# First attention of a two-block network on Trainium2: scores contracted over 128, 128 and 32 rows in place of three times 96

## The reference, cut to what matters

```
kv = (rms_norm(u_kv) @ w_kv_up);  k_nope, v = split(kv)        # 64 + 64 for each of 8 heads
q_rope = apply_rope(q_rope, cos, sin);  k_rope = apply_rope(u_kr, cos, sin)   # 32 features
s = einsum("bqhd,bkhd->bhqk", q_nope, k_nope) + einsum("bqhd,bkd->bhqk", q_rope, k_rope)
p = softmax(s * scale);   o = einsum("bhqk,bkhd->bqhd", p, v)
```

## Time and profile before

| | us |
|---|---|
| median of 3 runs (2778.56 to 2780.07) | 2779.03 |
| the profiled execution's own time | 2780.26 |
| its span, first to last instruction | 2778.3 |
| PE busy (98% of the span) | 2726.2 |
| DVE busy (65%) | 1800.1 |
| ACT busy (45%) | 1259.2 |
| POOL busy (16%) | 439.2 |

### The profile page before, as it was taken

The page is one execution under the profiler, slowest core; times in us unless marked ns, Lnnn a source line. Parts: engine busy times, 40 slices in busy tenths (PEclk is TensorE's granted clock), DMA queues, the critical chain, the costliest instruction groups (busy, mean ns, idle before and its releaser), DMA issues.

```text
span 2778.3 us, 36356 instructions
## 1 busy us (share of the span) xinstructions
PE 2726.2 (98%) x14436; PEld 2281.4 (82%) x14436; DVE 1800.1 (65%) x2497; ACT 1259.2 (45%) x2026; POOL 439.2 (16%) x393
## 2 busy tenths in 40 slices
PE   8999999999999999999999999999999999999998
PEld 7978888788884888888888887878888868888898
DVE  3646888330546888888885968988886572110575
ACT  4333787141432777777776124454454453111101
POOL 1500231000011211111102000000001043221341
PEclk9999999999999999999999999999999999999999
DMA  4041000420217999999982121030121221110141
GB/s 140 31 154 46 31 1 1 165 93 32 92 67 294 391 396 396 396 396 396 395 326 69 61 104 49 20 118 28 60 72 42 94 76 46 46 46 31 60 145 61
DMA packets 141604, 379.79 MB, mean 137 GB/s; under 512 B 11952, under 2 KB 45234, under 8 KB 141309
## 3 DMA queue, kind: packets, MB, share of 16 engines
q1 hardware_dynamic: 126140, 325.22, 30.9%
q0 software_dynamic: 12560, 42.74, 4.9%
q10 hardware_dynamic: 2736, 9.50, 0.9%
HBM read 341.13 MB, written 35.26 MB: 135 GB/s over the span
## 4 chain that ended last, share of the span: by engine, by line
PE 91%; DVE 4%; ACT 2%; DMA 1%; issue 1%; POOL 0%; SPq 0%; ACTq 0%; POOLq 0%; DVEq 0%
PE ps L2988 8%; PE ps L2989 8%; PE ps L2990 8%; PE ps L2591 7%; PE ps L2973 6%; PE ps L2975 6%; PE ps L2974 6%; PE ps L3082 3%; PE ps L3084 3%; PE ps L3083 3%; PE ps L2605 3%; PE ps L3129 2%; PE ps L3094 1%; PE ps L3096 1%; PE ps L3095 1%; PE ps L3114 1%
## 5 line engine op out<-in xcount | busy, mean ns | idle before, releaser
L2310 DVE SCALAR_TENSOR_TENSOR b_f<-b_f,small_f 128x1023 f32<-128x1023 f32 (+14 forms) x240 | 304.3, 1268 | 27.0 <-ACT small_f L1279 13.8
L2988 PE MATMUL ps<-x_f32r,w_f32r 128*128 128x512 f32 x480 | 187.9, 392 | 4.3 <-DVE b_f L2507 3.6
L2990 PE MATMUL ps<-x_f32r,w_f32r 128*128 128x512 f32 x480 | 187.4, 390 | 0.0
L2974 PE MATMUL ps<-w_f32r,a_f32r 128*128 128x512 f32 x456 | 177.4, 389 | 0.0
L2989 PE MATMUL ps<-ht_f32r,w_f32r 128*128 128x512 f32 x416 | 162.5, 391 | 0.0
L3083 PE MATMUL ps<-w_f32r,a_f32r 128*128 128x512 f32 x384 | 149.9, 390 | 0.0
L2974 PE MATMUL ps<-x_f32r,a_f32r 128*128 128x512 f32 x312 | 121.4, 389 | 0.0
L1279 ACT ACTIVATE x_f<-ps 128x512 f32<-128x512 f32 (+1 forms) x184 | 91.0, 533 | 44.4 <-PE ps L2591 21.0
L1209 POOL TENSOR_TENSOR w_f32r<-w_f,w_f32r 128x2048 fp32r<-128x2048 f32 x23 | 110.2, 4793 | 1.9
L2988 PEld LDWEIGHTS ps<-x_f32r,w_f32r 128*128 128x128 f32 x480 | 90.4, 188 | 23.7 <-issue 4.9
L2990 PEld LDWEIGHTS ps<-x_f32r,w_f32r 128*128 128x128 f32 x480 | 90.5, 189 | 18.9
(11 more groups left out here) (578 smaller groups left out, 7870.6 us busy)
## 6 DMA issues: line engine op xcount, KB each, us to landing
w_f<-in_w_exp_up SPq DMA_DIRECT2D x40, 1024.0 KB, 10.3
w_f<-in_w_exp_down SPq DMA_DIRECT2D x38, 1024.0 KB, 10.2
w_f<-in_w_exp_gate SPq DMA_DIRECT2D x36, 1024.0 KB, 8.8
x_f<-in_w_exp_gate SPq DMA_DIRECT2D x28, 1024.0 KB, 8.6
x_f<-in_w_exp_down SPq DMA_DIRECT2D x26, 1024.0 KB, 11.0
x_f<-in_w_exp_up SPq DMA_DIRECT2D x24, 1024.0 KB, 10.3
w_f<-in_w_in SPq DMA_DIRECT2D x22, 1024.0 KB, 5.1
w_f<-in_w_in SPq DMA_DIRECT2D x10, 2048.0 KB, 8.1
```

The costliest lines, as they stand in the source:

```text
L2310: ins = v.scalar_tensor_tensor(C_conv[k][:, d:S], U_conv[k][:, 0:S - d], cols[:, k, R_TAP + j:R_TAP + j + 1], C_conv[k][:, d:S], ALU.mult, ...
L2974: mm(o, x1, w2[:, k, c], start=False, stop=False)
L2988: mm(o, l1, r1, start=(k == 0), stop=False)
L2990: ins = mm(o, l2, r1, start=False, stop=(k == n - 1))
```

## The change

The same 288 rows of products for each score are laid out anew. The first matmul contracts 128 rows: the high query's nope rows twice, against the key's low nope rows (rows 0 to 63) and its high nope rows (64 to 127). The second contracts 128 rows: the query's low nope rows and twice its high rope rows, against the key's high nope rows and its high and low rope rows. The third contracts 32 rows: the query's low rope rows (`r_lo`) against the key's high rope rows (`s_hi`), which lie four times in `s_hi`, at partitions 0, 32, 64 and 96. The two matmuls of 32 rows of a step stand at different partitions (0 and 32 for an even head, 64 and 96 for an odd one) and write to different banks. In the built program they carry a tile size of 32 rows by 128 columns, where the others have 128 by 128.

The second copies of high rows are made by transfers between places of the on-chip memory (`upper`, `lower`, `doubled`). POOL makes 14 copies of 32 by 512 in place of 2 of 32 by 3584. ACT and DVE split the rotated queries for all heads at once (`rope_round` and the loop behind it).

```diff
         def head_parts(nm, h):
             if nm == "k":
-                return KT[:, h, :], k_hi[h % 2], KT_lo[:, h, :]
-            return QT[:, h, :], q_hi[h % 2], QT_lo[:, h, :]
+                return KT[:, h, :], (k_hi[h % 2][0:NOPE, :], k_both[NOPE:P, h, :]), k_both[0:NOPE, h, :]
+            return QT[:, h, :], (q_hi[h % 2][0:NOPE, :], q_hi[h % 2][NOPE:P, :]), q_rest[0:NOPE, h, :]
@@ SP, under "mkv0"
-                    for j in range(2):
-                        sp.wait_ge(sem("q_rope"), j + 1)
-                        for m in range(2):
-                            sp.dma_start(QT[...head 0, half j...], rope_out[m][0:16, c]).then_inc(sem(f"q_first{j}"), 16)
+                    sp.wait_ge(sem("q_rope"), 4)
+                    def upper(h, name):
+                        for m in range(2):
+                            for r in (NOPE, NOPE + ROPE):
+                                sp.dma_start(value(q_rest[r + 16 * m:r + 16 * m + 16, h, :]), value(rope_hi[m][16 * h:16 * h + 16, :])).then_inc(sem(name), 16)
+                    def lower(h, name):
+                        for m in range(2):
+                            for r in (NOPE * (h % 2), NOPE * (h % 2) + ROPE):
+                                sp.dma_start(value(r_lo[h // 2][r + 16 * m:r + 16 * m + 16, :]), value(rope_lo[m][16 * h:16 * h + 16, :])).then_inc(sem(name), 16)
+                    upper(0, "q_first"), lower(0, "q_first")
                     for h in range(1, H1):
-                        (2 transfers of QT's rope rows, q_rest)
+                        upper(h, "q_rest")
+                    sp.wait_ge(sem("q_first"), 16 * 8)
+                    sp.wait_ge(sem("q_rest"), 16 * 4 * (H1 - 1))
+                    for h in range(1, H1):
+                        lower(h, "q_rest")
+                    def doubled(h):
+                        for j in range(2):
+                            sp.wait_ge(sem("head_hi"), 2 * h + 2 + j)
+                            lower_rows, upper_rows = head_parts("kq"[j], h)[1]
+                            sp.dma_start(value(upper_rows), value(lower_rows)).then_inc(sem("q_rest"), 16)
+                    doubled(1), doubled(2)
                     bk.wait(sp, ("s1", 2 * T - 1))
                     (2 transfers of w_out)
+                    for h in range(3, H1):
+                        doubled(h)
@@ POOL
+            bk.wait(pool, ("vt", T - 1))
             for j in range(2):
                 bk.read(pool, ("kr", j))
-                nc.gpsimd.tensor_copy(KT[NOPE:HD1, 1:H1, c], ...).then_inc(sem("k_rope"), 1)
+                for r in range(ROPE, P, ROPE):
+                    nc.gpsimd.tensor_copy(s_hi[r:r + ROPE, c], value(s_hi[0:ROPE, c]))
+                for i in range(2):
+                    nc.gpsimd.tensor_copy(k_hi[i][NOPE:HD1, c], value(s_hi[0:ROPE, c]))
+                    ins = nc.gpsimd.tensor_copy(k_hi[i][HD1:P, c], value(s_lo[:, c]))
+                ins.then_inc(sem("k_rope"), 1)
@@ ACT
+                if h == 0:
+                    nc.scalar.activation(hi[1][:, c], whole[:, c], ACT.Copy)
+                nc.scalar.activation(hi[0][:, c], whole[:, c], ACT.Copy).then_inc(sem("head_hi"), 1)
+            def rope_round(h):
+                act.wait_ge(sem("k_rope"), 2)
+                act.wait_ge(sem("q_rope"), h + 1)
+                for m in range(2):
+                    ins = nc.scalar.activation(rope_hi[m][:, NB * h:NB * h + NB], rope_out[m][...], ACT.Copy)
+                ins.then_inc(sem("rope_hi"), 1)
+            rope_round(0)
             for c, h in QF[:4]:
                 heads_copy(("qf", c, h), QT, c, h, HD1 ** -0.5)
+                if (c, h) == (0, 0):
+                    rope_round(1)
             for j in range(2):
-                act.wait_ge(sem(f"q_first{j}"), 32)
                 head_hi("q", 0, slice(NB * j, NB * j + NB))
@@ DVE, behind the two rounds
+            for h in range(2):
+                dve.wait_ge(sem("rope_hi"), h + 1)
+                for m in range(2):
+                    ins = v.tensor_tensor(rope_lo[m][:, c], rope_out[m][:, c], value(rope_hi[m][:, c]), ALU.subtract)
+                ins.then_inc(sem("q_rope"), 1)
@@ PE, the scores of a step
+                    if n == 0:
+                        pe.wait_ge(sem("k_rope"), 2)
+                        pe.wait_ge(sem("q_first"), 16 * 8)
+                    if t == 0 and h >= 1:
+                        pe.wait_ge(sem("q_rest"), 16 * 8 * (H1 - 1) + 32 * h)
-                    for j in range(2):
-                        c = slice(NB * j, NB * j + NB)
-                        mm(PS[:, b + j, :], q1, k_hi[h % 2][:, c], start=True, stop=False)
-                        mm(PS[:, b + j, :], q1, KT_lo[:, h, c], start=False, stop=False)
-                        ins = mm(PS[:, b + j, :], q2, k_hi[h % 2][:, c], start=False, stop=True)
+                    for j in range(2):
+                        mm(PS[:, b + j, :], q_hi[h % 2][:, tile(t)], k_both[:, h, halves[j]], start=True, stop=False)
+                    for j in range(2):
+                        mm(PS[:, b + j, :], q_rest[:, h, tile(t)], k_hi[h % 2][:, halves[j]], start=False, stop=False)
+                    for j in range(2):
+                        r = NOPE * (h % 2) + ROPE * j
+                        ins = mm(PS[:, b + j, :], r_lo[h // 2][r:r + ROPE, tile(t)], s_hi[r:r + ROPE, halves[j]], start=False, stop=True)
```

More of the change, by code:

```diff
@@ L615, in build @@
         pq = mem(HT0, 8192).rearrange("p (c r m k) -> p c r m k", c=4, r=8, m=2)
[L616 to L620, removed]
+        KT, QT = (mem(at_, 8192)[0:NOPE, :].rearrange("p (h s) -> p h s", h=H1) for at_ in (HT0, GA0))
+        k_both, q_rest = (mem_r(at_, 8192).rearrange("p (h s) -> p h s", h=H1) for at_ in (HT0, GA0))
+        k_hi, q_hi = ([mem_r(GC0 + at_ + 1024 * i, 1024) for i in range(2)] for at_ in (0, 2048))
+        s_hi = mem_r(HN_AT + 1024, 1024)
+        s_lo = mem_r(SPARE, 1024)[0:ROPE, :]
+        rope_hi, rope_lo = ([mem_r(at_ + 1024 * m, 1024) for m in range(2)] for at_ in (SPARE, up_slot["kvup"]))
+        r_lo = [mem_r(at_, 1024) for at_ in (up_slot["kvup"] + 2048, up_slot["kvup"] + 3072, SPARE, SPARE + 1024)]
         Vr = mem_r(X0, 8192).rearrange("p (t h m d) -> p t h m d", t=T, h=H1, m=2)
@@ L1100, in _ @@
                     whole, hi, lo = head_parts("kq"[(t - 3) // 2], h + 1)
-                    nc.gpsimd.tensor_tensor(lo, whole, value(hi), ALU.subtract).then_inc(sem("head_lo"), 1)
+                    nc.gpsimd.tensor_tensor(lo, whole, value(hi[0]), ALU.subtract).then_inc(sem("head_lo"), 1)
                 if i >= 35 and i % 2 and i <= 41:
@@ L1388, in head_hi @@
                 whole, hi, lo = head_parts(nm, h)
-                nc.scalar.activation(hi[:, c], whole[:, c], ACT.Copy).then_inc(sem("head_hi"), 1)
+                if h == 0:
+                    nc.scalar.activation(hi[1][:, c], whole[:, c], ACT.Copy)
+                nc.scalar.activation(hi[0][:, c], whole[:, c], ACT.Copy).then_inc(sem("head_hi"), 1)
             bk.read(act, ("kf", 0, 0)), bk.read(act, ("kf", 0, 1))
@@ L1403, in mix_round @@
                 bk.read(act, ("o1", 8 * c + 7))
+                if c == 0:
+                    act.wait_ge(sem("q_rest"), 16 * 8 * (H1 - 1))
                 nc.scalar.activation(mixa_hi[:, c, :], mixa[:, c, :], ACT.Copy).then_inc(sem("mix_hi"), 1)
@@ L1417, in _ @@
                     if i == 1:
-                        act.wait_ge(sem("k_rope"), 2)
-                        act.wait_ge(sem("q_rest"), 16 * 2 * (H1 - 1))
                         for c, u in KF:
@@ L2005, in head_low @@
                 whole, hi, lo = head_parts(nm, 0)
-                v.tensor_tensor(lo[:, c], whole[:, c], value(hi)[:, c], ALU.subtract).then_inc(sem("block1_lo"), 1)
+                v.tensor_tensor(lo[:, c], whole[:, c], value(hi[0])[:, c], ALU.subtract).then_inc(sem("block1_lo"), 1)
             for c, h in KF:
@@ L2017, in _ @@
             for j in range(2):
+                c = slice(NB * j, NB * j + NB)
+                bk.wait(dve, ("rt", 1, 1))
                 b = bk.wait(dve, ("kr", j))
-                bk.done(v.tensor_copy(KT[NOPE:HD1, 0, NB * j:NB * j + NB], PS[0:ROPE, b, :]), ("kr", j))
+                ch(v.tensor_copy(s_hi[0:ROPE, c], PS[0:ROPE, b, :]))
+                bk.done(v.tensor_tensor(s_lo[:, c], PS[0:ROPE, b, :], value(s_hi[0:ROPE, c]), ALU.subtract), ("kr", j))
             for t in range(T):
```

8 lines of the change are left out of this document (3 added, 5 removed).

## The result

The changed kernel takes 2811.08 us in the median of 4 runs (2810.08 to 2812.02); on the same chip the kernel before takes 2779.39 (2778.56 to 2780.07). The ratio is 1.0114, with a 95% interval of 1.0097 to 1.0132. The profiled execution took 2811.09 us with a span of 2809.3, 31.0 more than before. The forecast was 2820 (2797 to 2838): direction, order of the terms and mechanism held, two terms were too large, and one was 1.4 too small.

The account below looks back on a forecast made before the run. PE, busy 98% of the span, was taken to set the pace. Step 8 22.0, clock 2.6, 56 steps 11.8 and heads 2 to 7 4.5 sum to 40.9 on 2780.26: 2821.2, as median 2820 us (2797 to 2838).

Parts of the forecast that it names:

- Step 8 later: Head 1's start: step 8 waits for SP's queued transfers and starts at 314.2 instead of 292.23, +22.0 us.
- Half clock behind it: After PE's stop at step 8, PE works at half clock for 5.3 us, losing 2.6 us (bounds 0 to 3.5).
- Steps: Attention loop: tiling change in and out +0.44, pair overlap -0.23, so +0.21 a step; 56 steps, +11.8 us.
- Heads 2 to 7: Start of each new head: PE waits for the second copy's transfer, +0.75 for each of six, +4.5 us (0 to 8).
- POOL, DVE, ACT, SP, step 0: Chain into the loop: POOL's 14 copies, rotation, splits, transfers; step 0 at 274.4 instead of 266.91, within the 22.0.
- Rival 2: POOL's copies change the type and cost 1.3 each: +9.4 on the whole chain, 2829 us; chance 0.12.
- The way in: In a step, from full matmuls into 32-row tiling: weight load not ahead of time, data late by 0.19 us.
- Going out: late by 0.25: In a step, from the 32-row pair back to full tiling: the next full matmul's data come 0.25 us late.
- landing in 3.5: Second-copy transfers of 256 KB land 3.5 us after issue (bounds 2.8 to 4.1); used for all new heads.
- Rival 1: Steps: slower, but the array changes its tiling free of charge, 56 x -0.23; +18.8 in sum, 2798 us; chance 0.10.
- Rival 3: Steps: the 32-row pairs do not overlap, +12.9 less 1.4 from shorter head waits, 2831 us; chance 0.07.
- Rival 4: SP's queue ahead of step 8: not slower, transfers stay hidden if an issue costs under 0.38; -4.6, 2774 us; chance 0.04.

Follow-up runs that it names:

- the second kernel: Changed kernel with the two 32-row matmuls replaced by two of 128 rows, so six full matmuls a step: 2806.89 us, ratio 1.0098 to before.

## Why the prediction was right, and which terms were too large

| Term | Forecast | Measured | How |
| --- | --- | --- | --- |
| Step 8 later | +22.0 | +23.4 | 315.59 against 314.2 |
| Half clock behind it | +2.6 | +2.1 | step 8 to step 9: 6.49 against 4.42 |
| Steps | +11.8 | +3.8 | 55 x 0.07, from pairs of 6.75 and 6.89 |
| Heads 2 to 7 | +4.5 | +1.7 | what is left; the step that ends with a new head's first score takes 2.86 (2.75 to 3.16) against 2.52, 0.11 of it tiling |
| Sum | +40.9 | +31.0 | |

**POOL, DVE, ACT, SP, step 0: right.** The copies took 0.61 each and ended at 255.5, the rounds ended at 260.7 and 264.7 (forecast 260.9 and 265.0), the first transfer went at 267.3 (267.6), step 0 began at 274.45 (274.4). Rival 2, copies that change the type at 1.3, is out: they do change the type (they are called CAST), and take 0.61. What the run without the wait adds is that this part is worth 5.8 us, all of it on the path through step 8.

**Step 8: right in its chain, 1.4 early.** The 28 uppers were issued by 290.4 (forecast: last at 289.9), the stop lasted until 292.44 (292.2), and then one issue took 1.82 us instead of 0.59: the last lower went at 310.69 instead of 309.4. It isn't part of the change: the kernel with the third product at 128 rows issued its last transfer at 310.29, where the changed one did at 311.97, with the longest issue at 0.80 (0.5 of the difference is that its SP began that much earlier). Where the profile of before has 14 issues, all between 577 and 598 ns, a queue of 66 is long enough to meet one that isn't. Head 1's last copy then took 3.5 us to land, as forecast, and PE started.

**The clock: right.** PE stood still from 302.5 to 315.6. The granted clock fell to 0.50 at 306.3 and rose again at 320.0, so 4.4 us of PE's work ran at half of 2.4 GHz behind step 8. The stretch behind step 0 (0.50 from 268.8 to 279.0) cost nothing, hidden by the wait at step 8, as the forecast has it.

**A step costs 0.07, not 0.21: this is the term that was mis-sized**, by 8.0 us of the 9.9 in all. Three of its four parts stand. The way in is 0.20 (0.19 taken), the pair overlaps fully (-0.23), 128 rows cost what 96 did (the second kernel). The step that failed is "Going out: late by 0.25". It is 0.10 too large, in two halves. First, the forecast let the last 64-row matmul end 0.06 after its start, half of a full one's time. But two of a pair overlap because each runs its whole time beside the other: in that row the pairs start 0.112 apart, as the full 128-column matmuls do with 0.109. So the data of the last pair stream until 1713.51 and not 1713.46, and the next ones come in at 1713.71, late by 0.20; the kernel that changes the tiling twice has 0.19 there. Second, that figure was read where 64-row matmuls of 128 columns are followed by one of 512 columns. Here transposes follow, whose first is held for 0.05 and not for 0.10, and the way out is 0.15. That makes 0.20 + 0.15 - 0.23 = 0.12 on the short step, measured 0.11. The rest was not in the working at all: I took the added time as wholly exposed, because PE is busy 98%. But in the long step PE already waited 0.087 in its transposes for a bank, counted as busy time since the matmuls there last longer, and most of the addition went into this wait (+0.03). So the mean is 0.07. Of the 8.0 us some 5.5 belong to the way out, and 2.4 to the wait.

By the Trainium skill's page "TensorE: Matmul & The Clock Gate", Part 3, each further row tile of a pack adds some 4 ns; the 3 ns between the two starts agree. The page has no price for going into the pack and out of it, and the 0.35 here are more than the 0.23 that a pack of two saves.

**Heads 2 to 7: +1.7, not +4.5.** The failed step is "landing in 3.5". The second copies, from their own line (count, first and last start), then from issue to landing for head 1's two, and for the others:

```profile
L956 SPq DMA_DIRECT2D ht_f32r<-c_f32r x7: 461/462/590, 311.3 to 476.9; - x7
...
DMA to landing us min/median/max: 3.0/3.3/3.5
...
DMA to landing us min/median/max: 2.8/2.8/3.1
```

I worked the 3.5 out with the queues busy for 0.64 of the time, which is head 1's case, and there it was 3.5. I carried it to the later heads, where the queues are nearly idle (0.01 in the earlier trace rows), and there it is 2.8, the lower bound. The mechanism is the one that was forecast, though a reader of the profile has to look twice. ACT, SP, POOL and PE at the start of a head:

```profile
397.98 1.05 ACT L1422 ACTIVATE c_f32r<-a_f 64x1024 fp32r<-64x1024 f32 x1
...
399.05 0.46 SPq L956 DMA_DIRECT2D c_f32r<-c_f32r  x1
...
399.11 2.37 POOL L1132 TENSOR_TENSOR a_f32r<-a_f,c_f32r 64x1024 fp32r<-64x1024 f32 x1 [4.50 <-ACT c_f32r L1422]
...
401.90 0.19 PEld L2824 LDWEIGHTS ps<-ht_f32r,c_f32r 128*128 128x128 f32 x1 [0.46 <-POOL a_f32r L1132]
```

The load's idle time is put down to POOL, but POOL is done at 401.48, 0.42 before PE starts. The copy was issued at 399.05, and with its 2.8 us it lands at 401.85: PE waits for the transfer. In before the same wait ends 0.05 after POOL's instruction.

**The rivals.** Rival 1, a tiling change free of charge, is out: the steps are 0.07 longer each, where it has them 0.23 shorter. The range, whose lower end was drawn for it, holds the time all the same, since what I missed lies on its side. The forecast's own range of 2811 to 2830 holds 2811.08 only at its very edge. That is luck: it was drawn from the heads, the transfers and the clock, and the steps' term, the one most wrong, had no share in it. Rival 3 was the experiment on the same rows, and would have cost the 13 us that it names. Rival 4, not slower, was refuted where it said it would be decided: an issue costs 0.63, not 0.38. Even with the better order of transfers and the early rotation the change stays 11 to 14 us above before: steps 8 to 63 take 194.1 instead of 188.55 (4 of tiling, the rest mostly the heads), and step 8 starts 5.5 us late (297.7), since head 0's eight transfers and head 1's ten still stand between the rotation and the scores, and 3.4 us of the work behind step 0 runs at half clock. The other 2.1 us of this profile lie behind the loop, where the granted clock is 0.50 for 21.8 us against 18.1 in before. The changed kernel's own profile has 18.1 there too, so this is no part of the change. No kernel tried here beats the one before.

## What to carry to other kernels

A change that saves PE nothing can lose its time far from PE: here 18 of 31 us came from the order in which one queue issues 64 small transfers and from a copy that stood ahead of work that did not need it, so lay the issues of the new path out on the time axis (count x pitch) and compare with when the consumer gets there. Price a change of the array's tiling by its way in and its way out at the very neighbours it will have, and ask whether the step has another limit close behind, seen in matmuls that last longer than their kind, before multiplying a loss per step by the number of steps. A transfer's landing time belongs to the load of the queues at its moment; take it from there, not from the nearest row of the same size.

## What the runs showed of the hardware that was not expected

- Two 32-row matmuls on different rows start 3 ns apart and last 0.49 together; on the same rows they last 0.72, and four in two such pairs 0.73. A pair costs the time of one matmul wherever it stands in such a stretch.
- The way out of 32-row tiling depends on what follows: 0.15 us into transposes of 128 columns, 0.19 into matmuls of 512 columns.
- 64 KB between two places on the chip landed 2.3 to 2.4 us after issue while SP alone issued. When POOL and SP issued four each in the same 2 us, POOL's landed in 3.1 to 5.5 and SP's in 2.6 to 5.7: a second queue gave nothing. The Trainium skill's page "DMA: Bandwidth & Descriptors", Anatomy of one DMA, fits 2.0 us and bytes at 436 GB/s for GpSimd's path, which would be 2.15; beside SP's the measurement is 3.1 at the least, and it decides. SP's 2.3 to 2.4 lie near the fit.
- 256 KB took 2.8 us to land on idle queues, and 3.5 behind the 64 KB transfers.
- In some of the kernels a single one of SP's 66 issues took 1.4 to 1.8 us where 0.59 is usual, each time at another place (294.9 here, 295.9 in the kernel that changes the tiling twice, 288.4 in the one with the early rotation); what causes it stays open. These three came 2 to 4 us behind the stop in SP's queue. The kernel with head 1's transfers first had one of 1.59 elsewhere in the queue, the one in which POOL issues too had two (1.58 and 1.70), and the kernels with the pair on the same rows and with the third product at 128 rows had none above 0.86.
